# A decoder layer's early program in another order: keys of half the tokens taken together with their index queries

## The chip, the cores and the metric

The kernel runs on one core of one Trainium2 chip. The metric is device time in microseconds (us) of one execution. The core has five engines with instruction queues of their own, each worked off strictly in order: TensorE (PE in the profile, PEld for its weight loads), VectorE (DVE), ScalarE (ACT), GpSimd (POOL) and SyncE (SP), which here only issues transfers. Engines meet at semaphores. Matmuls write into PSUM banks, from which VectorE and ScalarE read.

## The reference

One decoder layer over 1024 tokens of width 1024. An adaLN modulation of the condition `c` gives shift, scale and gate; the RMS-normalised tokens times scale plus shift (`h`) go through one wide projection, whose columns feed a pooling branch and a sparse-attention branch.

```python
mod = silu(c) @ w_ada + b_ada
shift, scale, gate = split(mod, 3)
h = rmsnorm(x, norm_gain) * (1 + scale) + shift
proj = h @ w_in          # u_a z_a | q k v z_b | q_idx k_idx w_idx | g_a g_b
k, q: rmsnorm by head, partial rotary; q_idx, k_idx: partial rotary
score = sum over heads of relu(q_idx . k_idx) * w_idx    # causal; top 256 keys per query
attn = softmax over the selected keys of q . k, times v
x = x + gate * ((sigmoid(g_a) * (y_a @ w_branch_a) + sigmoid(g_b) * (y_b @ w_branch_b)) @ w_out)
```

All of it is float32.

## The kernel before

Tokens are held in 8 tiles of 128 (`NT`), channels in 8 blocks of 128 (`KD`). For float32 accuracy each operand of a large product is split into a rounded part and the remainder (`hT_hi`, `hT_lo`; `w_hi`, `w_lo`), and a product is three matmuls: hi x hi, hi x lo, lo x hi. ScalarE makes the rounded parts. VectorE makes the remainders of the tokens, and the remainders of weight pieces are made by VectorE or GpSimd (`split_piece_v`, `split_piece_lo`).

The order of the work is written out by hand, one list per engine. Three lists say who uses the PSUM banks and in which order: `pp_uses` (two banks), `pt_uses` (two, for transposes) and `ps_uses` (two double banks). A user claims a bank, which waits until the engine that read the last tenant has freed it. Weights come in pieces of 512 channels by 256 columns through three buffers `w_raw`; a load waits for the remainder of the piece three before it.

The early program, which the change rewrites, goes like this. Token tiles arrive, ScalarE takes the sum of squares of each (`square`), TensorE transposes them block by block (`h_transposes`; blocks 0 to 7 are channels of tokens 0 to 511, `f` = 0, blocks 8 to 15 those of tokens 512 to 1023, `f` = 1), and ScalarE copies the result back over `x_in` (`x_turned`). The scale part of the modulation is a product of `silu(c)` with 8 blocks of `w_ada`: VectorE folds most of them into a running sum `ada_acc` (`ada_product`), TensorE does two with one-column matmuls (`scale_columns`), and TensorE adds over partitions (`modulation_sums`). `keep_warm` is idle matmuls between them.

Keys, values, the indexer's key and its head weights (200 columns, `kv`) are computed on tokens that are scaled but not yet normalised or shifted: `scaled_hi` and `scaled_lo` make the parts, `kv_half(0)` and `kv_half(1)` do four token tiles each, ScalarE multiplies by the reciprocal root of the tile (`kv_tiles`), and a row that stands for the shift (`r`, from `shift_b`) is added to all eight tiles at once (`kr`). Meanwhile VectorE folds all 8 shift blocks (`shift_fold`), which come through four buffers `shift_w`. Only then the true tokens are made, all 16 blocks: `normalised` on VectorE, `ht_hi` on ScalarE, `ht_lo` on VectorE; the roots reach it as rows (`root_row`) by way of TensorE (`root_rows`). The index queries follow (`qi_pairs` for tiles 2, 3 and 4, 5 at 512 columns, `rows_tile` for tiles 6 and 7 at 256), then the first four tiles of q, and at L906 the index scores of block 2, which VectorE weights and sums (L2017, L2020) after it has finished the keys. Tiles 0 and 1 need no index queries, since they have at most 256 keys.

GpSimd makes the remainders of the four index-query pieces and of `wg_raw`, then the rotary of the index queries tile by tile (`rope`).

## Time and profile before

| | |
|---|---|
| median of 3 runs | 833.2 us (828.48 to 833.89) |
| profiled execution | 823.55 us |
| its span, first to last instruction | 821.8 us |
| mean granted TensorE clock in it | 0.994 of full |
| TensorE, VectorE, ScalarE, GpSimd busy | 97%, 72%, 44%, 44% of the span |

Times in all views are from the start of the span. A row of a timeline gives start, duration, engine, line, operation and, in brackets, how long the engine sat idle before it and what released it. A busy share of TensorE is of pipelined matmuls whose ends are modelled, so that starts, not durations, give the pace of a row of matmuls.

### The profile page before, as it was taken

The page shows a single profiled execution, that of the slowest core. Times are in us where ns is not written, and L with a number is a line of the kernel's source. Part 1 is how long each engine was busy: PE and PEld are TensorE (multiplying, and loading weights), DVE is VectorE, ACT ScalarE, POOL GpSimd, SP SyncE. Part 2 cuts the span into 40 slices and gives each one's busy share as a digit, 9 for nine tenths or more (in the row PEclk, how much of TensorE's full clock was granted, in tenths as well). Part 3 has the DMA queues.
Part 4 walks back from the last instruction along what each step waited for, and adds up shares of the span by engine and source line. Part 5 has one row for each costly group of instructions (what it writes and reads, how often), then busy time and mean ns, then how long its engine had stood idle before and what let it go on. Part 6 is the DMA issues. An engine that isn't in the chain of part 4 may idle for free.

```text
span 821.8 us, 12753 instructions
## 1 busy us (share of the span) xinstructions
PE 796.1 (97%) x4389; PEld 674.4 (82%) x4393; DVE 587.7 (72%) x1213; ACT 360.9 (44%) x657; POOL 358.0 (44%) x316
## 2 busy tenths in 40 slices
PE   6979999999999999999999999899999999999998
PEld 4878897888888888887778887788888887888987
DVE  5889658977888888888888716556667885772522
ACT  5866356674232222222342212587777883330100
POOL 1033844333444477852752211765888811540000
PEclk9989999999999999999999999999999999999999
DMA  9841030004242220331123321743433114753431
GB/s 343 322 140 44 7 98 14 26 14 123 93 145 65 91 79 30 97 102 52 52 76 103 103 78 67 243 143 126 134 112 109 47 27 138 256 170 123 130 101 58
DMA packets 59368, 87.87 MB, mean 107 GB/s; under 512 B 5513, under 2 KB 36525, under 8 KB 59310
## 3 DMA queue, kind: packets, MB, share of 16 engines
q1 hardware_dynamic: 47954, 65.06, 25.4%
q10 hardware_dynamic: 9436, 15.75, 5.2%
q0 software_dynamic: 1920, 6.29, 2.0%
q8 instruction: 35, 0.57, 0.3%
q14 instruction: 23, 0.19, 0.1%
HBM read 66.12 MB, written 20.97 MB: 106 GB/s over the span
## 4 chain that ended last, share of the span: by engine, by line
PE 82%; DVE 8%; ACT 3%; issue 3%; DVEq 2%; DMA 1%; POOL 1%; ACTq 0%; POOLq 0%
PE pp L720 22%; PE pp L722 21%; PE pp L721 21%; PE pp L1107 3%; PE pt L1082 3%; PE ps L906 3%; PE ps L907 3%; DVE score L2020 1%; DVE ada_acc L1822 1%; DVE hT_lo L1913 1%; DVE x_in L1906 1%; DVE hT_lo L1865 1%; DVEq L1821 1%; DMA col_rows<-in_b_ada 1%; ACT w_hi L657 1%
## 5 line engine op out<-in xcount | busy, mean ns | idle before, releaser
L662 POOL TENSOR_TENSOR w_lo<-w_raw,w_hi 128x1024 fp32r<-128x1024 f32 x45 | 111.4, 2490 | 172.8 <-ACT w_hi L657 171.3
L2045 DVE TENSOR_SCALAR_CACHE_REDUCE junk<-score,cand 128x384 uint8<-128x384 f32 (+1 forms) x186 | 168.6, 944 | 19.3 <-issue 13.3
L720 PE MATMUL pp<-hT_hi,w_hi 128*128 128x512 f32 x384 | 150.2, 391 | 0.0
L722 PE MATMUL pp<-hT_hi,w_lo 128*128 128x512 f32 x384 | 149.5, 389 | 0.0
L721 PE MATMUL pp<-hT_lo,w_hi 128*128 128x512 f32 x384 | 149.5, 389 | 0.0
L720 PEld LDWEIGHTS pp<-hT_hi,w_hi 128*128 128x128 f32 x384 | 72.1, 188 | 15.9 <-issue 0.8
L722 PEld LDWEIGHTS pp<-hT_hi,w_lo 128*128 128x128 f32 x384 | 72.1, 188 | 15.2
L721 PEld LDWEIGHTS pp<-hT_lo,w_hi 128*128 128x128 f32 x384 | 72.1, 188 | 14.8
L2108 DVE TENSOR_TENSOR pT<-pt,pT 128x512 fp32r<-128x512 f32 (+3 forms) x96 | 50.6, 555 | 45.6 <-ACT pT L1498 42.4
L1382 ACT ACTIVATE stage<-pp 128x512 f32<-128x512 f32 x32 | 19.1, 598 | 126.7 <-PE pp L722 126.7
L657 ACT ACTIVATE w_hi<-w_raw 128x1024 fp32r<-128x1024 f32 x52 | 52.8, 1053 | 44.8 <-PE pp L722 40.9
L720 PE MATMUL pp<-w_hi,hT_hi 128*128 128x256 f32 (+1 forms) x208 | 69.2, 333 | 1.0 <-ACT qi L1244 0.5
L721 PE MATMUL pp<-w_lo,hT_hi 128*128 128x256 f32 (+1 forms) x208 | 67.4, 324 | 0.0
L722 PE MATMUL pp<-w_hi,hT_lo 128*128 128x256 f32 (+1 forms) x208 | 67.4, 324 | 0.0
L720 PE MATMUL pp<-w_hi,mT_hi 128*128 128x512 f32 (+1 forms) x160 | 55.6, 348 | 0.2 <-DVE o_row L2214 0.2
L721 PE MATMUL pp<-w_lo,mT_hi 128*128 128x512 f32 (+1 forms) x160 | 55.5, 347 | 0.0
L722 PE MATMUL pp<-w_hi,mT_lo 128*128 128x512 f32 (+1 forms) x160 | 55.5, 347 | 0.0
L720 PE MATMUL pp<-yT_hi,w_hi 128*128 128x512 f32 x128 | 52.6, 411 | 0.8 <-ACT a_out L1446 0.8
L2020 DVE SCALAR_TENSOR_TENSOR score<-rel,w_idx,score 128x384 f32<-128x384 f32 (+5 forms) x42 | 45.7, 1087 | 9.0 <-ACT rel L1343 5.4
L1506 ACT ACTIVATE prob<-prob,neg_max 128x128 f32<-128x128 f32 (+7 forms) x64 | 49.8, 778 | 3.3 <-DVE neg_max L2178 2.9
L2214 DVE TENSOR_TENSOR o_row<-pp,gate 128x512 f32<-128x512 f32 (+1 forms) x20 | 11.7, 583 | 54.3 <-PE pp L722 54.3
L722 PE MATMUL pp<-yT_hi,w_lo 128*128 128x512 f32 x128 | 50.1, 392 | 0.0
(297 smaller groups left out, 1841.4 us busy)
## 6 DMA issues: line engine op xcount, KB each, us to landing
w_raw<-in_w_in SPq DMA_DIRECT2D x36, 512.0 KB, 3.7
shift_w<-in_w_ada SPq DMA_DIRECT2D x8, 512.0 KB, 6.9
sgb_spill<-stage ACTq DMA_DIRECT2D x16, 256.0 KB, 2.0
sga_spill<-stage ACTq DMA_DIRECT2D x16, 256.0 KB, 2.0
stage<-sga_spill SPq DMA_DIRECT2D x16, 256.0 KB, 3.1
ma_spill<-stage POOLq DMA_DIRECT2D x16, 256.0 KB, 2.4
gate_w<-in_w_ada SPq DMA_DIRECT2D x16, 256.0 KB, 2.7
w_raw<-in_w_out SPq DMA_DIRECT2D x8, 512.0 KB, 4.2
```

The lines of the kernel that those rows point to most:

```text
L657: nc.scalar.activation(hi, raw, ACT.Copy).then_inc(w_hi_done, 1)
L662: nc.gpsimd.tensor_tensor(lo, raw, hi.bitcast(F32), ALU.subtract).then_inc(w_lo_done, 1)
L720: nc.tensor.matmul(o, a_hi, b_hi, start=first, stop=False)
L721: nc.tensor.matmul(o, a_hi, b_lo, start=False, stop=False)
L722: return nc.tensor.matmul(o, a_lo, b_hi, start=False, stop=last)
L906: nc.tensor.matmul(o[:, a:z], q, kt_[:, 0, a:z], start=True, stop=False)
L907: last = nc.tensor.matmul(o[:, a:z], q, kt_[:, 1, a:z], start=False, stop=True)
L1082: last = nc.tensor.transpose(o[:, (t % 4) * P:(t % 4 + 1) * P], prob[j % 4][:, t * P:(t + 1) * P], ident[:])
L1506: nc.scalar.activation(prob[j % 4][:, 0:keys(b)], prob[j % 4][:, 0:keys(b)], ACT.Exp, scale=-1.0, bias=neg_max[:, j % 4:j % 4 + 1], accum_ ...
L2020: ins = v.scalar_tensor_tensor(s, rel[:, n % 2, 0:keys(b)], w, s, ALU.mult, ALU.add)
L2045: v.tensor_scalar(junk[:, n % 2, 0:keys(b)], score[:, score_at(b):score_at(b + 1)], least, None, ALU.is_ge, ALU.add, accum_out=cnt[:, n:n ...
L2108: v.tensor_tensor(pT[:, j // 2 % 2, t0:t1, 1, j % 2, :], pt[n % 2][:, 0:(t1 - t0) * P].rearrange("p (t q) -> p t q", q=P), pT[:, j // 2 % ...
```

## The change

Keys of token tiles 0 to 3 are made as before, on scaled tokens (`free_keys`), and only these four get the shift's row. Tiles 4 to 7 wait for their true tokens; then keys and index queries of the four tiles are computed together, channel block by channel block (`keys_and_queries`), keys in one double bank, two query tiles in `pp` and two in the other double bank (`qi67`). `scaled_hi`, `scaled_lo` of tokens 512 to 1023 no longer exist; the true tokens of `f` = 1 are made before those of `f` = 0. Index queries of tiles 2 and 3 come after, at 256 columns.

Around it: positions are the first load, and the angles of the rotary are computed before the column parameters arrive. Shift blocks have a place each (`shift_far` lies where half of `hT_lo` will be), so their loads wait for nothing; blocks 0 to 3 are loaded ahead of token tiles 4 to 7. TensorE does two of the shift's eight blocks (`shift_columns`, blocks 3 and 4), VectorE six. The roots of all eight tiles are taken in one step, and GpSimd copies them into `root_row`. The remainders of the four index-query pieces, of `wg_raw` and of the two pieces of q's first chunk are made by VectorE and not by GpSimd, and the index-query pieces alternate between the two chunks. ScalarE takes the sines early. Four keep-warm matmuls are left out.

```diff
+    pieces[2:6] = [(1, 0), (2, 0), (1, 1), (2, 1)]
...
-    QI_PAIRS = [2, 4]
-    QI_SINGLE = [(0, 6), (0, 7), (1, 6), (1, 7)]
-    pp_uses += [("kv", 0, t) for t in (0, 1, 4, 5)]
-    pp_uses += [("qi", BOTH, t + j) for t in QI_PAIRS for j in range(2)]
+    QI_SINGLE = [(0, 2), (0, 3), (1, 2), (1, 3)]
+    pp_uses += [("kv", 0, t) for t in (0, 1)]
+    pp_uses += [("qi", BOTH, t) for t in (4, 5)]
...
-    ps_uses = [("scale", "v"), (("kv2", 0), "a"), ("shift", "v"), (("kv2", 1), "a")]
+    ps_uses = [("scale", "v"), ("kv2", "a"), ("shift", "v"), ("kv4", "a"), ("qi67", "a"), ("r", "v")]
...
+        def shift_block(k):
+            if k < 4:
+                return shift_w[:, k, :].rearrange("p (a q) -> p a q", a=2)
+            return shift_far[:, 2 * (k - 4):2 * (k - 4) + 2, HALF:2 * HALF]
...
+            for k in range(4):
+                load_shift(k)
             for t in range(NT // 2, NT):
                 load_x(t)
-            for k in range(4):
-                load_shift(k)
-            load_piece(2)
             for k in range(4, KD):
                 load_shift(k)
-            load_piece(3)
-            load_piece(4)
+            for n in range(2, 5):
+                load_piece(n)
...
-            keep_warm(8)
+            keep_warm(4)
...
+            def shift_columns(o, i):
+                k = SHIFT_PE[i]
+                pe.wait_ge(shift_in[k], 16)
+                w = shift_block(k)
+                for j in range(KD):
+                    nc.tensor.matmul(o[:, i * KD + j:i * KD + j + 1], w[:, j // 4, (j % 4) * P:(j % 4 + 1) * P],
+                                     c_silu[:, k:k + 1], start=True, stop=True)
...
+            def keys_and_queries():
+                keys4, queries2 = ps_claim("kv4"), ps_claim("qi67")
+                o_kv = [keys4[:, (j // 2) * HALF + (j % 2) * KR_W:(j // 2) * HALF + (j % 2 + 1) * KR_W] for j in range(4)]
+                o_qi = [pp[pp_bank[pp_at[("qi", BOTH, 4 + j)]]][:] for j in range(2)]
+                o_qi += [queries2[:, 0:HALF], queries2[:, HALF:2 * HALF]]
+                first_piece = pieces_through[name_of["kv"]]
+                for k in range(KD):
+                    def tok(j):
+                        return slice((4 + j) * P, (5 + j) * P)
+                    def key_hi(j):
+                        nc.tensor.matmul(o_kv[j], hT_hi[:, k, tok(j)], kv_hi[:, k, :], start=k == 0 and j % 2 == 0, stop=False)
+                        nc.tensor.matmul(o_kv[j], hT_hi[:, k, tok(j)], kv_lo[:, k, :], start=False, stop=False)
+                    def query_hi(j):
+                        nc.tensor.matmul(o_qi[j], hT_hi[:, k, tok(j)], w_hi[:, :, k, :], start=k == 0, stop=False)
+                        nc.tensor.matmul(o_qi[j], hT_hi[:, k, tok(j)], w_lo[:, :, k, :], start=False, stop=False)
+                    def key_lo(j):
+                        return nc.tensor.matmul(o_kv[j], hT_lo[:, k, tok(j)], kv_hi[:, k, :], start=False,
+                                                stop=k == KD - 1 and j % 2 == 1)
+                    def query_lo(j):
+                        return nc.tensor.matmul(o_qi[j], hT_lo[:, k, tok(j)], w_hi[:, :, k, :], start=False,
+                                                stop=k == KD - 1)
+                    pe.wait_ge(hT_hi_done, KD + k + 1)
+                    if k == KD - 1:
+                        pe.wait_ge(hT_lo_v, KD + k + 1)
+                        for j in range(4):
+                            key_hi(j)
+                            last = key_lo(j)
+                            if j == 3:
+                                last.then_inc(ps_full, 1)
+                            query_hi(j)
+                            last = query_lo(j)
+                            if j < 2:
+                                last.then_inc(pp_full, 1)
+                            if j == 3:
+                                last.then_inc(ps_full, 1)
+                        continue
+                    for j in range(4):
+                        key_hi(j)
+                    if k % 4 == 0:
+                        pe.wait_ge(w_lo_done, first_piece + 2 * (k // 4) + 2)
+                    for j in range(4):
+                        if k == 0 and j < 2:
+                            pp_claim(("qi", BOTH, 4 + j))
+                        query_hi(j)
+                    if KD + k + 6 < 2 * KD:
+                        h_transposes(KD + k + 6)
+                    if k == 2:
+                        root_rows(0)
+                    pe.wait_ge(hT_lo_v, KD + k + 1)
+                    for j in range(4):
+                        key_lo(j)
+                        query_lo(j)
...
+            free_keys()
+            modulation = ps_claim("shift")
+            h_transposes(KD)
+            h_transposes(KD + 1)
+            shift_columns(modulation, 0)
+            h_transposes(KD + 2)
+            h_transposes(KD + 3)
+            shift_columns(modulation, 1)
+            root_rows(1)
+            modulation_sums(modulation, KD * len(SHIFT_PE), 1)
+            h_transposes(KD + 4)
+            h_transposes(KD + 5)
+            keys_and_queries()
...
+                if (i, t) == (0, 3):
+                    pe.wait_ge(shift_lo, 1)
+                    o = ps_claim("r")
+                    for k in range(KD):
+                        last = product(o[:, 0:KR_W], shift_b[:, 0, k, :], shift_b[:, 1, k, :], kv_hi[:, k, :],
+                                       kv_lo[:, k, :], k == 0, k == KD - 1)
+                    last.then_inc(ps_full, 1)
...
+            act.wait_ge(dve_ready, V_MEAN)
+            nc.scalar.activation(rx[:], ssx[:], ACT.Sqrt).then_inc(sqrt_done, 1)
+            for n in range(KD, KD + 4):
                 x_turned(n)
-                if n in ROOT_ROWS:
-                    o = pt_take(("R", ROOT_ROWS[n]))
-                    nc.scalar.activation(root_row[:, ROOT_ROWS[n], :], o[:], ACT.Copy).then_inc(pt_free_a, 1)
-                if n == KD:
-                    kv_tiles(0)
-                if n == KD + 1:
-                    split_piece_hi(act, 2)
-                if n == KD + 2:
-                    sqrt_half(1)
-                if n == KD + 5:
-                    split_piece_hi(act, 3)
+            split_piece_hi(act, 2)
+            root_taken(1)
+            free_key_tiles()
+            split_piece_hi(act, 3)
+            act.wait_ge(mod_done, 2)
+            ht_hi(KD)
+            x_turned(KD + 4)
+            x_turned(KD + 5)
+            ht_hi(KD + 1)
+            x_turned(KD + 6)
             split_piece_hi(act, 4)
-            act.wait_ge(dve_ready, V_SIN)
-            nc.scalar.activation(trig[:], reduced[:], ACT.Sin).then_inc(trig_done, 1)
-            act.wait_ge(mod_done, 2)
+            ht_hi(KD + 2)
+            x_turned(KD + 7)
+            root_taken(0)
+            ht_hi(KD + 3)
+            split_piece_hi(act, 5)
...
+            pool.wait_ge(dve_ready, V_RSQRT)
+            for f in (1, 0):
+                gp.tensor_copy(root_row[:, f, :].rearrange("p (t q) -> p t q", q=P),
+                               rx[:, 4 * f:4 * f + 4].unsqueeze(2).to_broadcast([P, 4, P])).then_inc(root_wide, 1)
...
+            FOLD_AFTER = {2: 0, 4: 1, 6: 2}
...
+            dve.wait_ge(ssx_done, NT)
+            v.tensor_scalar(ssx[:], ssx[:], 1.0 / D, EPS, ALU.mult, ALU.add).then_inc(dve_ready, 1)
+            shift_fold(5)
+            dve.wait_ge(sqrt_done, 1)
+            rsqrt_step(rx[:], ssx[:], nx[:])
+            v.tensor_copy(nx[:], rx[:]).then_inc(dve_ready, 1)
+            shift_fold(6)
+            for i in range(2):
+                shift_fold(7, (i,)).then_inc(ada_sum, 1)
...
+            split_piece_v(2)
+            normalised(KD)
+            dve.wait_ge(ps_full, ps_value("shift"))
+            sums = ps[ps_at["shift"] % 2][:, 0:PARTS * KD].rearrange("p (i j) -> p j i", i=PARTS)
+            v.tensor_reduce(shift[:, 0:KD], sums, AX.X, ALU.add).then_inc(ps_free_v, 1)
+            dve.drain()
+            v.tensor_tensor(shift[:, 0:KD], shift[:, 0:KD], col[:, 12:12 + KD], ALU.add).then_inc(mod_done, 1)
+            split_piece_v(3)
+            normalised(KD + 1)
+            ht_lo(KD)
+            normalised(KD + 2)
+            ht_lo(KD + 1)
+            split_piece_v(4)
+            normalised(KD + 3)
+            ht_lo(KD + 2)
+            split_piece_v(5)
+            normalised(KD + 4)
+            ht_lo(KD + 3)
             dve.wait_ge(shift_hi, 1)
             v.tensor_tensor(shift_b[:, 1, :, :], shift[:, 0:KD].unsqueeze(2).to_broadcast([P, KD, P]),
                             shift_b[:, 0, :, :].bitcast(F32), ALU.subtract).then_inc(shift_lo, 1)
-            for n in range(2 * KD):
-                if n + 2 < 2 * KD:
-                    normalised(n + 2)
+            for n in range(KD + 4, 2 * KD):
+                if n + 1 < 2 * KD:
+                    normalised(n + 1)
                 ht_lo(n)
+            normalised(0)
...
+            for n in range(2):
+                split_piece_v(pieces_through[name_of[("qi", 1)]] + n)
+            dve.wait_ge(ps_free_a, ps_done[ps_at["kv4"]][0])
+            dve.wait_ge(ps_full, ps_value("r"))
```

TensorE, the end of the keys on scaled tokens and what follows. Before, between the channel blocks of `kv_half(1)` (`pt` takes transposes, `ps` and `pp` the sums; L839 is the lo part of a block, L797 the shift's sums):

```order
L839 MATMUL pp<-kv_hi,hT_lo 128x200 x2
L839 MATMUL ps<-kv_hi,hT_lo 128x200 x2
L776 MATMUL pt<-ident,x_in 128x128 x4
L797 MATMUL ps<-ones,ada_acc 128x1 x8
L834 MATMUL ps<-kv_hi,hT_hi 128x200
```

Now, from the end of `free_keys` to the first of `keys_and_queries` (L868 is a key, L872 a query):

```order
L841 MATMUL ps<-kv_hi,hT_lo 128x200 x2
L785 MATMUL pt<-ident,x_in 128x128 x8
L853 MATMUL ps<-c_silu,shift_w 128x1 x8
L785 MATMUL pt<-ident,x_in 128x128 x8
L853 MATMUL ps<-c_silu,shift_far 128x1 x8
L791 MATMUL pt<-ident,root_row 128x128 x4
L806 MATMUL ps<-ones,ada_acc 128x1 x8
L785 MATMUL pt<-ident,x_in 128x128 x8
L868 MATMUL ps<-kv_hi,hT_hi 128x200
```

Transposes and sums of the second half stood between blocks of keys; now six groups of transposes, two shift products and the sums stand in one row.

SyncE, from the last load of key weights on. Before:

```order
L513 DMA w_raw<-in_w_in 128x4x128
L517 DMA x_in<-in_x 128x1024 x4
L521 DMA shift_w<-in_w_ada 128x1024 x4
L513 DMA w_raw<-in_w_in 128x4x256
L521 DMA shift_w<-in_w_ada 128x1024 x4
L513 DMA w_raw<-in_w_in 128x4x256 x2
```

Now:

```order
L522 DMA w_raw<-in_w_in 128x4x128
L528 DMA shift_w<-in_w_ada 128x1024 x4
L526 DMA x_in<-in_x 128x1024 x4
L528 DMA shift_far<-in_w_ada 128x2x512 x4
L522 DMA w_raw<-in_w_in 128x4x256 x3
```

Token tiles 4 to 7 moved behind four shift blocks, and the first query piece behind all eight.

ScalarE, the scaled blocks of channels 2 to 7 (L1248) and the squares of token tiles 4 to 7 (L1237), in the new program:

```order
L1248 ACTIVATE hT_hi<-x_in,gmul 128x512 x2
L1237 ACTIVATE w_lo,ssx<-x_in 128x1024
L1248 ACTIVATE hT_hi<-x_in,gmul 128x512
L1237 ACTIVATE w_lo,ssx<-x_in 128x1024
L1248 ACTIVATE hT_hi<-x_in,gmul 128x512
L1237 ACTIVATE w_lo,ssx<-x_in 128x1024
L1248 ACTIVATE hT_hi<-x_in,gmul 128x512 x2
L1237 ACTIVATE w_lo,ssx<-x_in 128x1024
```

Squares stand between scaled blocks as before, but their tiles now arrive behind the shift blocks, and a scaled block waits behind each.

ScalarE a little later in the new program, from the second query piece's rounded part (L663) to the fifth true block (L1253); L1243 is a turned block, L1311 the second root rows:

```order
L663 ACTIVATE w_hi<-w_raw 128x1024
L1253 ACTIVATE hT_hi<-x_in,shift 128x512
L1243 ACTIVATE x_in<-pt 128x4x128 x2
L1253 ACTIVATE hT_hi<-x_in,shift 128x512
L1243 ACTIVATE x_in<-pt 128x4x128
L663 ACTIVATE w_hi<-w_raw 128x1024
L1253 ACTIVATE hT_hi<-x_in,shift 128x512
L1243 ACTIVATE x_in<-pt 128x4x128
L1311 ACTIVATE root_row<-pt 128x512
L1253 ACTIVATE hT_hi<-x_in,shift 128x512
L663 ACTIVATE w_hi<-w_raw 128x1024
```

The turned blocks, which came one by one with a scaled block each, now stand between the true blocks, and so do the roots and two weight pieces.

## Rows read from the trace of the kernel before

**Rows 1.** waits of TensorE over the span: total us, times, longest

```profile
PE pp L839 <- DVE hT_lo L1865: 3.9, 3, 1.8
```

**Rows 2.** timeline of TensorE: start, duration, line, out<-in, count, idle before

```profile
19.28 1.07 PE L776 MATMUL pt<-ident,x_in 128*128 128x128 f32 x8
...
27.77 0.28 PE L834 MATMUL ps<-kv_hi,hT_hi 128*128 128x200 f32 x1
...
29.11 0.27 PE L834 MATMUL ps<-kv_hi,hT_hi 128*128 128x200 f32 x1
...
39.07 0.66 PE L776 MATMUL pt<-ident,x_in 128*128 128x128 f32 x4 [0.92 <-ACT kr L1235]
...
70.76 0.39 PE L874 MATMUL pp<-w_hi,hT_hi 128*128 128x512 f32 x1
...
72.12 0.39 PE L874 MATMUL pp<-w_hi,hT_hi 128*128 128x512 f32 x1
...
78.78 0.47 PE L874 MATMUL pp<-w_hi,hT_hi 128*128 128x512 f32 x1 [1.06 <-ACT qi L1244]
...
93.45 0.28 PE L720 MATMUL pp<-w_hi,hT_hi 128*128 128x256 f32 x1
...
96.33 0.46 PE L887 MATMUL pt<-ident_r,kst 128*128 128x128 f32 x4
...
115.84 0.34 PE L906 MATMUL ps<-kiT,qiT 128*128 128x384 f32 x1
```

**Rows 3.** chain that ended last, in order of time: start, us, what

```profile
21.31 1.67 PE pp L756 x7
22.99 1.69 PE ps L797 x16
...
55.05 2.83 PE ps L797 x16
...
66.13 0.66 DVE x_in L1906
```

**Rows 4.** timeline of VectorE, folds and the end of the keys

```profile
37.83 1.28 DVE L1822 SCALAR_TENSOR_TENSOR ada_acc<-shift_w,c_silu,ada_acc 128x1024 f32<-128x1024 f32 x1
...
41.98 3.29 DVE L1822 SCALAR_TENSOR_TENSOR ada_acc<-shift_w,c_silu,ada_acc 128x1024 f32<-128x1024 f32 x1
...
109.05 0.20 DVE L1805 RECIPROCAL rk<-rk 128x8 f32<-128x8 f32 x1 [13.20 <-ACT rk L1334]
...
117.44 1.10 DVE L2017 TENSOR_SCALAR score<-rel,w_idx 128x384 f32<-128x384 f32 x1 [0.57 <-ACT rel L1343]
```

**Rows 5.** timeline of GpSimd, a weight split

```profile
41.82 2.36 POOL L662 TENSOR_TENSOR w_lo<-w_raw,w_hi 128x1024 fp32r<-128x1024 f32 x1 [37.33 <-ACT w_hi L657]
```

**Rows 6.** timeline of VectorE, its start

```profile
9.84 0.21 DVE L1773 CAST pos_f<-pos_i 8x128 f32<-8x128 int32 x1 [6.71 <-DMA col_rows<-in_b_ada]
...
14.53 0.75 DVE L1820 TENSOR_SCALAR ada_acc<-scale_w,c_silu 128x1024 f32<-128x1024 f32 x1
```

**Rows 7.** windows: us, busy of PE, PEld, DVE, ACT, POOL, granted clock, DMA share, GB/s

```profile
8.00:10.00 2.00, 0.00 (x0) 0.00 (x0) 0.16 (x1) 1.84 (x5) 0.00 (x0) 1.00 1.03 415
...
52.00:54.00 2.00, 0.16 (x2) 0.08 (x1) 1.91 (x4) 0.47 (x1) 0.00 (x0) 1.00 0.48 104
...
56.00:58.00 2.00, 2.00 (x10) 2.00 (x11) 0.10 (x1) 1.98 (x3) 0.71 (x1) 0.50 0.00 0
```

**Rows 8.** DMA issues from 17 to 18 us: count, KB, us to landing

```profile
x_in<-in_x SPq DMA_DIRECT2D x1, 512.0 KB, 6.5
```

**Rows 9.** timeline of ScalarE, square and scaled block

```profile
28.65 1.04 ACT L1172 ACTIVATE hT_lo<-x_in 128x1024 fp32r<-128x1024 f32 x1
...
29.87 0.73 ACT L1191 ACTIVATE hT_hi<-x_in,gmul 128x512 fp32r<-128x512 f32 x1
30.50 1.04 ACT L1172 ACTIVATE hT_lo<-x_in 128x1024 fp32r<-128x1024 f32 x1
```

**Rows 10.** VectorE's instructions on one tile, later weight splits: ns min/median/max, first and last start

```profile
L1839 DVE TENSOR_TENSOR w_lo<-w_raw,w_hi x7: 1220/1224/1226, 193.7 to 776.8; 128x1024 fp32r<-128x1024 f32 x7
```

More of the change, by code:

```diff
@@ L226, in hybrid_layer @@
         pt_uses += [(key, "a") for key in QI_EXTRA.get(use, [])]
-    pt_uses += [(Q_EXTRA[n], "a") for n in Q_EXTRA]
+    pt_uses += [(key, "a") for n in Q_EXTRA for key in Q_EXTRA[n]]
     pt_uses += [(K_AFTER[h], "a") for h in K_AFTER]
@@ L424, in hybrid_layer @@
         ada_end = [sem(f"ada_end{i}") for i in range(2)]
[L425 removed]
+        shift_in = [sem(f"shift_in{k}") for k in range(KD)]
         mod_done, shift_hi, shift_lo = sem("mod_done"), sem("shift_hi"), sem("shift_lo")
@@ L829, in kv_half @@
-                    pe.wait_ge(hT_hi_done, KD * f + k + 1)
-                    for j in (2, 3, 0, 1):
-                        if k == 0 and j < 2:
-                            pp_claim(("kv", 0, 4 * f + j))
-                        tok = slice((4 * f + j) * P, (4 * f + j + 1) * P)
-                        nc.tensor.matmul(o[j][:, 0:KR_W], hT_hi[:, k, tok], kv_hi[:, k, :], start=k == 0, stop=False)
-                        nc.tensor.matmul(o[j][:, 0:KR_W], hT_hi[:, k, tok], kv_lo[:, k, :], start=False, stop=False)
@@ L836, in kv_half @@
-                    pe.wait_ge(hT_lo_v, KD * f + k + 1)
-                    for j in range(4):
-                        tok = slice((4 * f + j) * P, (4 * f + j + 1) * P)
-                        last = nc.tensor.matmul(o[j][:, 0:KR_W], hT_lo[:, k, tok], kv_hi[:, k, :], start=False,
+                    pe.wait_ge(hT_hi_done, k + 1)
+                    for t in (2, 3, 0, 1):
+                        if k == 0 and t < 2:
+                            pp_claim(("kv", 0, t))
+                        tok = slice(t * P, (t + 1) * P)
+                        nc.tensor.matmul(o[t][:, 0:KR_W], hT_hi[:, k, tok], kv_hi[:, k, :], start=k == 0, stop=False)
+                        nc.tensor.matmul(o[t][:, 0:KR_W], hT_hi[:, k, tok], kv_lo[:, k, :], start=False, stop=False)
@@ L840, in kv_half @@
+                    pe.wait_ge(hT_lo_v, k + 1)
+                    for t in range(4):
+                        tok = slice(t * P, (t + 1) * P)
+                        last = nc.tensor.matmul(o[t][:, 0:KR_W], hT_lo[:, k, tok], kv_hi[:, k, :], start=False,
                                                 stop=k == KD - 1)
-                        if k == KD - 1 and j < 2:
+                        if k == KD - 1 and t < 2:
                             last.then_inc(pp_full, 1)
                 last.then_inc(ps_full, 1)
+            def shift_columns(o, i):
[5 more added lines that the diff above has]
+                                     c_silu[:, k:k + 1], start=True, stop=True)
@@ L927, in _ @@
                 q_step(n)
-                if n % KD == KD - 1 and n // KD in Q_EXTRA:
-                    qi_transposes(FREE_BLOCKS, [Q_EXTRA[n // KD][2]])
+                if n % KD == KD - 1:
+                    for key in Q_EXTRA.get(n // KD, []):
+                        if key[0] == "ki":
+                            key_transposes(*key)
+                        else:
+                            qi_transposes(FREE_BLOCKS, [key[2]])
             for b in range(FREE_BLOCKS, NT):
@@ L1276, in _ @@
-            act.wait_ge(hT_lo_v, 4 * KD)
+            act.wait_ge(group_in, 16)
+            nc.scalar.activation(wg_hi[:], wg_raw[:], ACT.Copy).then_inc(wg_hi_done, 1)
+            for n in range(KD):
+                ht_hi(n)
             qi_tile(BOTH, 4)
             qi_tile(BOTH, 5)
+            late_key_tiles()
+            act.wait_ge(ps_full, ps_value("qi67"))
+            late = ps[ps_at["qi67"] % 2]
+            for j in range(2):
+                last = nc.scalar.activation(qi[:, 6 + j - FREE_BLOCKS, :], late[:, j * HALF:(j + 1) * HALF], ACT.Copy)
@@ L1280, in q_tile @@
+            last.then_inc(ps_free_a, 1)
             def q_tile(i, t):
@@ L1329, in _ @@
                 q_tile(i, t)
-                if n in Q_EXTRA:
-                    qi_copies(FREE_BLOCKS, [Q_EXTRA[n][2]])
+                for key in Q_EXTRA.get(n, []):
+                    if key[0] == "ki":
+                        key_copy(*key)
+                    else:
+                        qi_copies(FREE_BLOCKS, [key[2]])
                 if n == 0:
```

263 lines of the change are left out of this document (98 added, 165 removed).

## The prediction

> **What bounds the kernel now.** I first read the page's chain by engine, which is TensorE for the most part, then TensorE's waits. What it waits longest for on VectorE in the whole span is 3.9 us in three pieces, all in the key product, ahead of 55 us [rows 1]. From the first scores on (115.84 us [rows 2]) TensorE is close to full, and that part of the program is the same in both kernels. So the change is worth what it moves the start of the scores, if VectorE, which accumulates them, starts earlier too. I therefore rebuilt the stretch from 0 to 116 us from the timelines of the engines.
>
> In that stretch TensorE's steps have steady prices. One block of keys of four tiles is twelve matmuls, 27.77 to 29.11 us: 1.34, or 0.112 each. One block of two query tiles at 512 columns is six matmuls, 70.76 to 72.12: 1.36, or 0.227 each. One query tile at 256 columns is 93.45 to 96.33: 2.88. Two groups of f32 transposes take 1.07, a modulation product or sum with one-column matmuls (16 records) 1.69 [rows 2, 3]. VectorE's passes over a 128x512 block cost 0.66 [rows 3], a 1024-wide fold 1.28 [rows 4]. The same fold took 3.29 while GpSimd ran a weight split of 2.36 beside it [rows 4, 5]: four such splits fall into VectorE's early program.
>
> **The change part by part.** All times that follow are estimates on the clock of the profiled execution.
>
> Start. VectorE sits idle 6.71 us until 9.84 and then does some 3.4 us of angle work before its first modulation product at 14.53 [rows 6]. Positions now arrive first and the angles go into that idle time. But the products cannot gain 3.4: each wants a 0.52 MB block, and at 415 GB/s [rows 7] one lands every 1.26 us, as long as one product takes. I let them end 1 us earlier. TensorE has four keep-warm matmuls fewer (1.67 for seven: 0.95 [rows 3]), so both sides of the sum move together and the scale is ready at 24.2 and not 25.3. Bounds: 0.3 to 1.5 gained; I take 1.1.
>
> Free keys. The tokens' tiles 4 to 7 now queue on SP behind four shift blocks, 4 x 1.26 = 5 us. The first of them landed 6.5 us after its issue at about 17.1 [rows 8], at 23.6; now 28.7 to 29.4. ScalarE's squares of these tiles stand between its eight scaled blocks, and the engine comes to the first at about 27.5 (28.65 before [rows 9], less 1.1). It waits 1.2 to 1.9 there, and with it every block behind it on ScalarE, and TensorE's keys. From 29.5 ScalarE alone sets the pace: four squares at 1.22 (28.65 to 29.87) and four blocks at 0.63 (to 30.50 [rows 9]), the last block at 35.8. VectorE's last remainder and fold bring the end of the free keys to 38.4; before it was 38.15 (39.07 less 0.92 [rows 2]). The gain of the start is gone.
>
> Shift. Next TensorE does, in a row, six groups of transposes (0.53 each), one of the roots (0.4), two products of shift blocks that VectorE used to fold, and the sums: 3 x 1.69 of one-column matmuls. The sums end at 46.0. VectorE is not late: its folds 5, 6 and 7 (3.9), the roots (1.4) and the mean fit from 38.0 to 43.8. GpSimd's two root copies fall beside folds 6 and 7. No row has such a copy on GpSimd. The nearest is its split: 2.36 beside a fold that lost 2.0 [rows 4, 5], so 0 to 2 us on VectorE, of which what exceeds its slack comes on the path, at most 1.4. A copy reads one input and not two, so I stay near the low end, at 0.3. Then 0.5 for shift on VectorE and 0.65 for the first true block on ScalarE, behind its weight split: the first key matmul at 47.4.
>
> Keys and queries together. A block is 12 x 0.112 + 12 x 0.227 = 4.06, eight are 32.5, with two transposes and one of the roots 33.8. VectorE has per block two passes (1.32) and, four times in all, a split at 1.22 [rows 10], less than 4.06: TensorE sets the pace here, where VectorE did before. Two places in ScalarE's queue are new waits: turned block 14 waits for a transpose behind block 0's queries, the second roots for one behind block 2's. Behind the roots stand block 11 of the left operand, which TensorE wants at 60.3 and gets at about 60.2, and the split of the fourth query piece; behind that split stands VectorE. I take 0.4 lost, at most 0.8. End: 81.6. The blocks of the first half are finished on VectorE at about 80.2, before TensorE comes to them: no wait, with 1.4 to spare at the first tile and more at its last block.
>
> To the scores. Four query tiles, four tiles of q (8 x 2.88 = 23.0), the shift row (24 x 0.112 = 2.7), six groups of transposes at 0.3, and 0.5 for two key copies that now stand behind ScalarE's weight splits: 28.0. The hand-offs of the old order (1.06 at 78.78 [rows 2], and a shorter one) are gone, since the last block ends tile by tile. First scores at 109.6 against 115.84: **6.2 earlier**, 5.9 after GpSimd's copies.
>
> VectorE must follow. It waits for two splits of q pieces that ScalarE starts at 87.7 and for the shift row at 90; then the same key work as before runs. The key root on ScalarE comes at about 101.4 with no table load ahead of it, and VectorE needed 8.4 from there to its first score (109.05 to 117.44 [rows 4]): 109.8. Before it was ready at about the time when TensorE was, and so it is now.
>
> **The clock** is the term that no sum of works gives. Before, TensorE was busy 0.16 of 2 us from 52; then 0.50 was granted, 1.2 instead of 2.4 GHz, through the sums of one-column matmuls and into the keys [rows 7]. These sums took 2.83 instead of 1.69 [rows 3], and some 4.4 us of keys at half speed cost 2.2 more: 3.3 in all. In the new program the stretch from 38.4 to 47.4 holds 5.1 us of one-column matmuls between short transposes and ends in a wait of about a microsecond. I expect a fall here too, a shorter one: the dense matmuls come right after. Bounds 0 and 4; I take 2.
>
> The Trainium skill (TensorE: Matmul & The Clock Gate, What's actually happening) says that "the default state is throttled, and activity releases the throttle". Read as busy time, it would keep the clock up in the new stretch, where TensorE is nearly always busy, and the time would be the first rival's. The rows speak against that reading: from 56 to 58 TensorE was busy 2.00 of 2.00 us, in those very sums, at 0.50 [rows 7].
>
> **The sum.** 5.9 - 2 = 3.9 us. The profiled execution took 823.55 (span 821.8), so 819.6 there. The runs shown have their median 9.6 higher, at 833.2, and I carry the difference over: **829.3**, 0.5% faster. A difference under 1%, 8.3 us, can hardly be told from none here (the three runs lie 5.4 apart).
>
> **The rivals.**
> - The clock holds, or x tile 4 lands at the early end: 5.9 to 8 gained, 825 to 827.5. For it: the stretch has no pause as long as the 1.8 us before the old fall [rows 1]. Against it: the sums at 0.50.
> - The gain does not arrive: VectorE, not TensorE, sets when the scores go on, and its key work is delayed by GpSimd's rope passes of six blocks, which now all lie in its way from 82 to 99, or by the wait for the q splits, which stands ahead of it in its queue. With 3 to 4 us more there the gain is 0 to 2: 831 to 833. For it: VectorE's slack to the first score is only some tenths. Against it: it ran the same key work beside four rope passes before, and that is in its 8.4.
> - Slower: the late x tiles thin out the free keys so far that the clock already falls there. Keys at half speed take 2.68 a block, over ScalarE's 1.84, so four blocks lose 3.4; the shift's products and sums lose 3 x 1.14; the joint blocks 2.2. That is 9.0 against 6.2: 836. It decides from about 31 us, if the pauses there exceed 1.5 us each; I expect 0.5.
>
> **How the numbers follow.** Forecast 0.46 (2 to 5.9 gained, 827.3 to 831.2), clock holds 0.27, gain does not arrive 0.18, slower 0.09. Faster by over 1% needs 8.3 gained, beyond the best of the second case; with the spread of the runs I leave it 0.14. Slower by over 1% is the far part of the last case, 0.05. The rest, 0.81, is within 1%. For 8 in 10 the range goes from the good end of the second case, less some 1.5 for the spread of the medians, to a little beyond the third: 823.5 to 834.5.
>
> **What would show it.** Right: ScalarE's wait of over 1 us before the square of x tile 4, near 28; the free keys ending within 1 us of 38.4; the first joint block at 47 to 49; TensorE without gaps from there to 109 or 111; no 3 us folds. A granted clock of 0.50 between 42 and 52 confirms the clock's term; 1.0 there, with the scores at 109.6, is the first rival. Wrong: joint blocks longer than 4.2 us at full clock (then VectorE or ScalarE still sets the pace), TensorE waiting for VectorE at the first keys of the scores, or a fall of the clock at 30 us.

## The result and the profile after

The changed kernel took 823.29 us (median of 11 runs, 821.67 to 828.2), the kernel before 828.7 us over as many (826.43 to 833.89; the first three, shown above, happened to be high). The ratio is 0.9931 with the interval 0.9906 to 0.9956: 0.7% faster, 5.4 us. The forecast was 829.3 us with a range from 823.5, so the time lies 0.2 us below the range. The gain itself was forecast at 3.9 us.

The two profiled executions show no gain at all: 824.74 us after (span 823.0), 823.55 before. So the traces must first be compared step by step, and then it must be asked what the profiled execution of before stands for. Two rows of its TensorE, to be set beside those that follow: its pause ahead of 10 us and its first key.

```profile
10.11 0.24 PE L761 MATMUL pt<-ident,col_rows 28*128 28x28 f32 x1 [2.40 <-DVE pos_f L1773]
...
26.34 0.36 PE L834 MATMUL ps<-kv_hi,hT_hi 128*128 128x200 f32 x1 [0.57 <-DVE kv_lo L1839]
```

TensorE in the changed kernel, timeline (start, duration, line, tile, count, idle before):

```profile
4.78 3.17 PE L762 MATMUL pp<-prefix,ident_b 128*128 128x512 bf16 x7 [0.89 <-POOL rope_a L1646]
8.87 0.30 PE L771 MATMUL pt<-ident,col_rows 28*128 28x28 f32 x1 [0.92 <-DMA col_rows<-in_b_ada]
...
24.54 0.36 PE L836 MATMUL ps<-kv_hi,hT_hi 128*128 128x200 f32 x1 [0.57 <-DVE kv_lo L1907]
...
31.99 0.33 PE L836 MATMUL ps<-kv_hi,hT_hi 128*128 128x200 f32 x1 [1.84 <-ACT hT_hi L1248]
...
39.48 1.04 PE L785 MATMUL pt<-ident,x_in 128*128 128x128 f32 x8
...
46.11 3.41 PE L806 MATMUL ps<-ones,ada_acc 128*128 128x1 f32 x16
49.38 1.95 PE L785 MATMUL pt<-ident,x_in 128*128 128x128 f32 x8
50.98 0.52 PE L868 MATMUL ps<-kv_hi,hT_hi 128*128 128x200 f32 x1
...
57.18 0.26 PE L868 MATMUL ps<-kv_hi,hT_hi 128*128 128x200 f32 x1
...
61.73 0.26 PE L868 MATMUL ps<-kv_hi,hT_hi 128*128 128x200 f32 x1
...
69.91 0.36 PE L876 MATMUL ps<-kv_hi,hT_lo 128*128 128x200 f32 x1 [0.54 <-DVE hT_lo L1973]
...
87.82 0.28 PE L726 MATMUL pp<-w_hi,hT_hi 128*128 128x256 f32 x1
...
115.86 0.34 PE L963 MATMUL ps<-kiT,qiT 128*128 128x384 f32 x1
```

Between 8.87 us and the end of the early program TensorE hardly stops: the waits of [rows 1] and the hand-off of [rows 2] are gone. What is left above 0.6 us is one pause of 1.84 ahead of block 4 of the free keys. ScalarE's timeline names its cause, the late token tile, which holds the square and the scaled block behind it:

```profile
29.90 1.06 ACT L1237 ACTIVATE w_lo<-x_in 128x1024 fp32r<-128x1024 f32 x1 [2.96 <-DMA x_in<-in_x]
```

And yet the scores start at 115.86, as before [rows 2]. The windows (busy of PE, PEld, DVE, ACT, POOL, granted clock, DMA share, GB/s) show where the gain went:

```profile
30.00:32.00 2.00, 0.15 (x3) 0.04 (x1) 0.12 (x1) 1.92 (x4) 0.00 (x0) 1.00 1.01 394
...
34.00:36.00 2.00, 2.00 (x11) 2.00 (x11) 1.10 (x3) 1.92 (x4) 0.00 (x0) 0.50 1.05 387
...
42.00:44.00 2.00, 2.00 (x20) 2.00 (x21) 1.84 (x2) 1.27 (x3) 1.37 (x1) 1.00 0.11 29
44.00:46.00 2.00, 2.00 (x12) 2.00 (x12) 1.96 (x2) 0.76 (x1) 0.00 (x0) 0.52 0.00 0
...
50.00:52.00 2.00, 2.00 (x12) 2.00 (x11) 2.00 (x4) 1.84 (x4) 0.00 (x0) 0.50 0.00 0
```

The clock fell twice: after the pause, in the free keys, and again at 44.1 us, within the one-column matmuls of the shift, until 54 us. The sums took 3.27 (46.11 to 49.38) and joint block 0 took 6.20, against 4.55 for block 1. Both mechanisms were in the prediction, one as its clock term, one as the slower rival.

VectorE kept up. Its first score came 1.59 after TensorE's, before 1.60 [rows 2, 4], although two steps of eight elements, which take 0.17 elsewhere, took 1.33 and 2.27 beside two weight splits of GpSimd. Its rotary, which the second rival feared, had ended at 105.24. The kernel before has the same splits there and one such step of 2.06.

```profile
106.57 4.75 POOL L668 TENSOR_TENSOR w_lo<-w_raw,w_hi 128x1024 fp32r<-128x1024 f32 x2
...
107.67 1.33 DVE L1886 TENSOR_TENSOR nk<-rk 128x8 f32<-128x8 f32 x1
109.07 2.27 DVE L1888 TENSOR_TENSOR nk<-nk,ssk 128x8 f32<-128x8 f32 x1
...
117.45 1.10 DVE L2100 TENSOR_SCALAR score<-rel,w_idx 128x384 f32<-128x384 f32 x1 [0.87 <-ACT rel L1420]
```

Behind the first score the span has 707.1 us left, before 706.0. Most of the extra microsecond arises in one wait, at 519.68 on ScalarE's eqT (1.53; the wait at the same place before was 0.81), which stood behind a load of q rows that landed 1 us later after the same weight split. Why it landed later was not followed.

### The profile page after: what moved, and what is told of

The parts are those of the page before. It is cut to its first block, busy times and chain, and to the rows that moved or that the text cites. A ratio compares the mean times of both kernels' runs of the same rounds, so it can differ in the third digit from the quotient of the medians.

```text
span 823.0 us, 12776 instructions
## 1 busy us (share of the span) xinstructions
PE 802.8 (98%) x4421; PEld 680.7 (83%) x4421; DVE 580.0 (70%) x1201; ACT 351.6 (43%) x644; POOL 336.4 (41%) x311
## 4 chain that ended last, share of the span: by engine, by line
PE 83%; DVE 5%; ACT 4%; SPq 2%; issue 2%; DMA 2%; DVEq 1%; POOL 0%; ACTq 0%
PE pp L726 21%; PE pp L728 20%; PE pp L727 20%; PE pp L1173 3%; PE pt L1148 3%; DVE score L2103 2%; PE ps L963 2%; PE ps L964 2%; SPq L522 1%; DMA x_in<-in_x 1%; ACT w_hi L663 1%; DVE pT L2191 1%; DVE prob L2261 1%; PE pt L1081 1%; ACT rel L1420 1%
## 5 line engine op out<-in xcount | busy, mean ns | idle before, releaser
L668 POOL TENSOR_TENSOR w_lo<-w_raw,w_hi 128x1024 fp32r<-128x1024 f32 x39 | 96.4, 2487 | 122.3 <-ACT w_hi L663 121.0
L663 ACT ACTIVATE w_hi<-w_raw 128x1024 fp32r<-128x1024 f32 x52 | 52.8, 1053 | 44.6 <-PE pp L728 40.9
L1583 ACT ACTIVATE prob<-prob,neg_max 128x128 f32<-128x128 f32 (+7 forms) x64 | 49.8, 778 | 3.4 <-DVE neg_max L2261 2.9
L727 PE MATMUL pp<-yT_lo,w_hi 128*128 128x512 f32 x128 | 50.1, 391 | 0.0
```

The costliest lines, as they stand in the source:

```text
L663: nc.scalar.activation(hi, raw, ACT.Copy).then_inc(w_hi_done, 1)
L668: nc.gpsimd.tensor_tensor(lo, raw, hi.bitcast(F32), ALU.subtract).then_inc(w_lo_done, 1)
L727: nc.tensor.matmul(o, a_hi, b_lo, start=False, stop=False)
L1583: nc.scalar.activation(prob[j % 4][:, 0:keys(b)], prob[j % 4][:, 0:keys(b)], ACT.Exp, scale=-1.0, bias=neg_max[:, j % 4:j % 4 + 1], accum_ ...
```

## The experiments

The theory after this reading: the early program is shorter by about what was counted, and TensorE's clock, which falls in other places in other executions, decides what of it arrives. The rival: the 5 us lie elsewhere. Both kernels were profiled again, unchanged, beside edits.

**The kernel before, again.**

> The kernel before, unchanged, to see what an ordinary execution of it looks like: the profiled one took 823.55 us, the median of eleven is 828.7. Theory A (the two early programs differ by the works that were counted, and the rest is TensorE's clock, which falls in a different number of stretches from execution to execution): the executions at 826 to 829 have their first scores at 119 to 121 us, later than the 115.84 of the profile shown, by a longer or a second fall of the clock ahead of 116 us; mean clock 0.988 or below. Rival B (the 5 us lie elsewhere: in the scores, in the transfers, or ahead of the first instruction): first scores again near 116 us and clock near 0.994, and the added time comes after 116 us.

Median 827.34 (12 runs, 823.34 to 829.88). Its profile, of 826.33 us, has the first scores at 118.59, 2.75 later than in the execution shown and a little ahead of A's 119, and 706.0 us behind them: A and not B. But the loss is ahead of the keys, where the granted clock was 0.50 from 17.3 to 24.1 us, and the theory did not name that place: the first key is at 29.14 instead of 26.34. The executions near 828.5 have a mean clock of 0.996, higher than the quick ones (0.994), against A's 0.988. What those are was still open.

**The changed kernel, again.**

> The changed kernel, unchanged, to see how far its executions differ. Theory A: the clock falls in the keys on scaled tokens and again from the shift's products into the first joint block, as in the profile shown (first scores 115.86 us), or in only one of the two, and the first scores then come at 111 to 114; ratio to before 0.992 to 0.996. Rival B: the first scores stay within 0.5 us of 115.86 whatever the clock does, because VectorE sets them.

Median 823.58 (821.42 to 829.28); ratio 0.9945 (0.9917 to 0.9974). In this profile the fall lies in the start (the second scale product takes 3.41, first key 27.08) and in the shift (from 43.5 to 53.8 by the windows), not in the free keys; first scores 115.10, against A's 111 to 114. So where the clock falls differs between executions of one kernel.

**Tiles and shift blocks loaded in turns.**

```diff
             for k in range(4):
+                load_x(4 + k)
                 load_shift(k)
-            for t in range(NT // 2, NT):
-                load_x(t)
```

> The changed kernel with the loads of token tiles 4 to 7 and shift blocks 0 to 3 taking turns, instead of all four shift blocks ahead of the tiles. Tile 4 should land near 25 us and not 29.9. Theory A: ScalarE no longer waits 2.96 us ahead of the square of tile 4, TensorE's pause of 1.84 us at block 4 and the fall of the clock from 33.7 to 37.1 us are gone, the keys on scaled tokens end at 36 to 37 us and not 39.5, and the scores and the whole come 2 to 3 us earlier than in the changed kernel, unless VectorE's folds become late. Rival B: VectorE's folds or ScalarE set the end of the shift's sums in any case, the free keys end earlier and the sums do not: 0 to 0.5 us.

In the profile ScalarE runs from the scaled blocks into the square with no wait (first fence), TensorE's pause is gone, the free keys end at 35.71 instead of 39.48, and the scores start at 110.56. That is A's mechanism, and 5.3 us earlier, where A had 2 to 3; 3.8 of them are there at the end of the free keys. The median is 823.16 (818.82 to 828.54), 0.4 under the changed kernel on the same chip: a gain that one execution shows and twelve don't measure.

```profile
26.63 1.04 ACT L1236 ACTIVATE w_lo<-x_in 128x1024 fp32r<-128x1024 f32 x1
```

```profile
35.71 1.04 PE L784 MATMUL pt<-ident,x_in 128*128 128x128 f32 x8
...
45.40 0.52 PE L867 MATMUL ps<-kv_hi,hT_hi 128*128 128x200 f32 x1
```

**The pause of the free keys filled.**

```diff
+                    if k == 4:
+                        for _ in range(8):
+                            nc.tensor.matmul(pt[0][:], ident_b[:], prefix[:, 0:512], start=True, stop=True)
                     pe.wait_ge(hT_hi_done, k + 1)
```

> The changed kernel with eight idle matmuls of 512 columns in the pause of TensorE ahead of block 4 of the keys on scaled tokens (about 1.9 us of work in a pause of 1.84). Theory A: the pause is what lets the clock fall at 33.7 us; filled, the keys of blocks 5 and 6 run at 0.112 us a matmul and not 0.215, the free keys end 0.5 to 1 us earlier, and the whole is 0 to 1 us faster. Rival C (the fall there comes from the slow pace of the keys and not from the pause): the clock falls all the same, and the time is the same.

The profile has no fall there; the free keys run at full speed and end at 37.96. Median 823.68 (822.31 to 828.46), the same. As A says for the clock; but after_again had no fall there without the fill, so one profile does not prove it. Of all profiles of the new order this is the only one with full clock through the shift's sums (43.62 to 45.33, 1.71) and the transposes behind them, and so it shows the works that the prediction counted:

```profile
43.62 1.84 PE L806 MATMUL ps<-ones,ada_acc 128*128 128x1 f32 x16
45.33 1.07 PE L785 MATMUL pt<-ident,x_in 128*128 128x128 f32 x8
47.40 0.51 PE L871 MATMUL ps<-kv_hi,hT_hi 128*128 128x200 f32 x1 [1.00 <-ACT hT_hi L1256]
...
55.08 0.26 PE L871 MATMUL ps<-kv_hi,hT_hi 128*128 128x200 f32 x1
```

The first joint key is at 47.40, as predicted, and then block 0 takes 7.68 at half clock. From block 1 to the scores it is 58.68 in this run, in the changed kernel and in x_between alike.

**Dense matmuls between the one-column rows** (on x_between).

```diff
             shift_columns(modulation, 0)
+            dense(3)
...
             shift_columns(modulation, 1)
+            dense(3)
...
             h_transposes(KD + 5)
+            dense(3)
```

> The kernel with tiles and shift blocks loaded in turns (x_between), and three idle matmuls of 512 columns behind each of the two products of shift blocks and three ahead of the first joint block: 2.2 us more for TensorE, of which 1 us falls into the wait for the first true block. Theory A: the fall of the clock from about 43 to 49 us comes from the row of one-column matmuls; with dense work between them it does not come or comes later and shorter, the first joint block takes 4.4 us and not 6.5 in most executions, and the time is 0 to 2 us lower than that of x_between. Rival D (the fall comes from the one-column rows all the same, dense matmuls between them or not): the fall stays, and the time is 1 to 2 us higher.

Median 821.05 (818.22 to 829.88), ratio 0.9931 (0.9891 to 0.9971) against 0.9932 for x_between: no difference that can be told. In the trace the fall comes later and is shorter (46.4 to 49.8 by the windows, against 42.5 to 49.3), and block 0 takes 4.94 instead of 6.48, but counted from the end of the free keys it starts 1.7 later (11.43 against 9.69). A holds for the clock and not for the time.

**All shift blocks on VectorE** (on x_between).

```diff
-        SHIFT_PE = (3, 4)
+        SHIFT_PE = ()
...
```

> x_between with all eight shift blocks folded by VectorE, none by TensorE: 3.4 us less of one-column matmuls, 2.6 us more of folds. Theory A (the step of the prediction that VectorE is not late with six folds): the last fold ends near 44.7 us instead of 42.1, TensorE waits some 3 us for it ahead of the sums, and the first joint block starts within 1 us of that of x_between at full clock, later by 0.5 to 2; the clock falls all the same, because of the wait; time 0 to 2 us higher. Rival E (TensorE's one-column work alone set the sums): the sums end earlier, and the time is 1 to 3 us lower.

TensorE waits for the last fold, as A says, and the clock falls in that wait:

```profile
44.43 3.58 PE L805 MATMUL ps<-ones,ada_acc 128*128 128x1 f32 x16 [4.15 <-DVE ada_acc L1938]
```

Median 822.99 (821.8 to 828.14), ratio 0.9931 (0.9897 to 0.9964): the same as x_between. What TensorE saves in one-column matmuls it waits, and more: from the end of the free keys to the first joint key it is 12.78 us, against 9.69 in x_between and A's 0.5 to 2 more, and to block 1 it is 18.55 against 16.17. E falls. The two blocks on TensorE are worth 2.4 us between these two traces and nothing that the medians show.

**The kernel before, two more profiles.**

> The kernel before, unchanged: one more profile, to find an execution of the kind that takes 828 to 830 us with a mean clock of 0.996, half of all its executions. Theory A2 (TensorE's clock falls less often there, but another engine is slower in the early program): first scores at 120 to 122 us. Rival B: first scores near 116 us, and the 5 us lie behind them.

> The kernel before, unchanged: as the look before this one, for the same purpose and with the same two outcomes.

825.86 us and 829.6 us, first scores at 118.35 and 122.09: not B, and the second has A2's time. But it is no other engine that is slower there, as A2 says; it is TensorE itself. The second is of the ordinary kind. Timeline of its TensorE, and one window of its start:

```profile
4.54 3.17 PE L756 MATMUL pp<-prefix,ident_b 128*128 128x512 bf16 x7 [4.54 <-POOL rope_a L1567]
10.28 0.30 PE L761 MATMUL pt<-ident,col_rows 28*128 28x28 f32 x1 [2.57 <-DVE pos_f L1773]
...
14.26 3.41 PE L790 MATMUL ps<-c_silu,scale_w 128*128 128x1 f32 x16
...
20.22 3.41 PE L790 MATMUL ps<-c_silu,scale_w 128*128 128x1 f32 x16
...
26.62 2.89 PE L756 MATMUL pp<-prefix,ident_b 128*128 128x512 bf16 x7 [0.22 <-issue]
...
32.87 0.36 PE L834 MATMUL ps<-kv_hi,hT_hi 128*128 128x200 f32 x1 [0.58 <-DVE kv_lo L1839]
...
122.09 0.34 PE L906 MATMUL ps<-kiT,qiT 128*128 128x384 f32 x1
```

```profile
14.00:18.00 4.00, 4.00 (x21) 3.91 (x20) 3.60 (x7) 0.00 (x0) 0.00 (x0) 1.00 1.03 395
```

Both scale products take 3.41, where 1.84 is usual, and seven idle matmuls 2.89, where the execution shown has 1.67 [rows 3]. The first seven, at 4.54 or 4.78, take 3.17 in all six profiles of the two kernels. So TensorE begins at half speed, and here it stays there, through two rows of one-column matmuls, until the idle matmuls at 26.62. The first key is 6.5 us later. The clock column says 1.00 all the while: the slow start is not in it, and a mean clock of 0.996 belongs to an execution that is slower than one of 0.994.

The kernel before pauses 2.2 to 2.6 us ahead of 10 us in all four profiles, for the positions; the changed one 0.95 at most. The next four kernels ask whether that is it.

**The start of the kernel before filled, and nothing else.**

```diff
-            keep_warm(7)
+            keep_warm(13)
```

> The kernel before with 13 instead of 7 idle matmuls at its start, so that TensorE's pause of 2.2 to 2.6 us ahead of about 10 us is filled; nothing else of the change. Theory F (most of what the change gains is TensorE's speed in the first 30 us: in the profile shown the seven idle matmuls ahead of the scale's sums took 1.67 us, in the look before_fourth 2.89, with the two scale products at 3.41 each instead of 1.84, and the first key 6.5 us later; the pause is what keeps TensorE slow there): the first key comes at 26 to 27 us in the profile, the executions at 828 and above become rare, and the median falls by 2 to 5 us, to 824 to 826.5. Rival G (the speed at the start does not hang on that pause): the distribution stays, median 827 to 829.

F, inside its range: median 824.24 (822.81 to 824.95), ratio 0.9949 (0.9928 to 0.9969) to the kernel before. Above 826.5 us lie none of 12 executions; of the kernel before, on the same chip, 21 of 31.

```profile
4.54 4.75 PE L756 MATMUL pp<-prefix,ident_b 128*128 128x512 bf16 x13 [4.54 <-POOL rope_a L1567]
...
10.87 1.07 PE L776 MATMUL pt<-ident,x_in 128*128 128x128 f32 x8
...
12.42 1.84 PE L790 MATMUL ps<-c_silu,scale_w 128*128 128x1 f32 x16
...
20.30 2.43 PE L756 MATMUL pp<-prefix,ident_b 128*128 128x512 bf16 x7 [0.22 <-issue]
...
26.09 0.36 PE L834 MATMUL ps<-kv_hi,hT_hi 128*128 128x200 f32 x1 [0.58 <-DVE kv_lo L1839]
...
115.55 0.34 PE L906 MATMUL ps<-kiT,qiT 128*128 128x384 f32 x1
```

The six more take 1.58 after the first seven's 3.17: TensorE is at full speed before it pauses, and the scale products behind run at 1.84. The clock still falls afterwards in this execution, granted 0.50 from 18.4 to 21.8 us, and the idle matmuls at 20.30 took 2.43.

The fill does two things at once: it shortens the pause (to 0.85) and it makes the first row of dense matmuls longer (4.75 and not 3.17). Which of them counts was not separated, and the pause alone does not explain it. Of the six profiles of the changed kernel and its variants with seven idle matmuls and a pause of 0.95 at most, four run the eight transposes behind at half speed (1.94 us; pause_filled and dense_between after a pause of 0.27), two at full (1.07). In all three profiles with ten or thirteen idle matmuls they take 1.06 to 1.11.

**The changed kernel with the pause back.**

```diff
-            keep_warm(7)
+            keep_warm(3)
```

> The changed kernel with three instead of seven idle matmuls at its start, so that TensorE pauses about 2.6 us ahead of 8.9 us, as it did in the kernel before. Theory F: the executions at 826 and above become the most frequent, first key at 27 to 31 us, median 2 to 5 us higher than the 823.5 of the changed kernel, about level with the kernel before. Rival G: same median within 1 us.

Median 825.89 (822.95 to 830.37), 2.3 to 2.6 above the changed kernel and a ratio of 0.9979 (0.995 to 1.0008): level with the kernel before. Six of 12 lie above 826.5, against 4 of 23 of the changed kernel. F in kind; as the most frequent executions, not quite. The interval overlaps that of the changed kernel (0.9917 to 0.9974), and this edit too changes the first dense row, to three matmuls (1.46 us), with the pause: the run fits F and does not show it.

**The changed kernel with its start filled.**

```diff
-            keep_warm(7)
+            keep_warm(10)
...
-            keep_warm(4)
+            keep_warm(8)
```

> The changed kernel with ten instead of seven idle matmuls at its start (its pause there is 0.9 us) and eight instead of four ahead of the scale's sums. Theory F: executions above 826 us become rare, median 822 to 823.5; against before_start_filled it is then 1 to 4 us faster, which is what the rest of the change is worth. Rival G: the distribution stays as that of the changed kernel, or 0.5 to 1 us higher for the seven matmuls.

Median 822.17 (11 runs, 820.87 to 824.8), none above 826.5, ratio 0.9931 (0.9908 to 0.9955). F. Its scores start at 113.06, those of before_start_filled at 115.55.

```profile
24.11 0.36 PE L836 MATMUL ps<-kv_hi,hT_hi 128*128 128x200 f32 x1 [0.58 <-DVE kv_lo L1907]
...
113.06 0.34 PE L963 MATMUL ps<-kiT,qiT 128*128 128x384 f32 x1
```

The rest of the change is thus worth 2.1 us between the medians (824.24 to 822.17; the intervals of the two ratios overlap) and 2.5 between the traces. Of these 2.5, 2.0 lie ahead of the first key (26.09 against 24.11), where the clock of the other execution fell. From the first key to the scores the new order is 0.5 shorter (88.95 against 89.46), with the clock at 0.50 for 6.8 us in each, from 45.4 and from 56.0.

**Loads in turns, dense matmuls and the start filled.**

> dense_between (tiles and shift blocks loaded in turns, dense matmuls in the shift's rows) with the same fill at the start. Theory F: its four executions of twelve at 828.7 to 829.9 us disappear, the rest stays at 818 to 821.5, median 819.5 to 821. Rival G: they stay, median 821 to 822.

The executions at 828 and above are gone (818.08 to 823.8, 9 runs), but the median is 821.95, above F's range and inside that of G, whose reason fails. The ratio is 0.9921 (0.989 to 0.9951). The kernel has the lowest times of all kernels here and no median that can be told from the changed kernel's. Block 0 ends at 51.85 in its profile and at 51.88 in x_between's: the dense matmuls cost what they give.

## Why the prediction was wrong

**The step that failed** is in its sum: "The runs shown have their median 9.6 higher, at 833.2, and I carry the difference over". It took the distance between the profiled execution and the runs as a constant, outside the program and known from three runs. Neither holds.

The forecast lies 6.0 us above the measured time, and 4.5 of that is the choice of runs: over 11 runs the distance is 5.2, and the same sum would have said 824.8. No trace is of an execution of 833 or 834 us, so what makes those stays open.

And the distance is largely inside the program: it is TensorE's speed in the first 30 us, which differs between executions and which the change acts on. The prediction costed the start from one execution, in which TensorE ran at half speed only ahead of 7.7 us and from 11.0 to 14.4 us, at 1.1 us gained (0.3 to 1.5). The two profiles shown differ by 1.8 at the first key (26.34 to 24.54), but the other executions of before have it at 28.89, 29.14 and 32.87. Filling the start alone gave 4.3 us of the median (828.57 to 824.24), with nothing else of the change. With both starts filled 2.1 of the 5.4 us are left, so some 3.3 came from the start, where 1.1 was counted, and 2.1 from the rest, where 2.8 was (3.9 less 1.1). That the forecast gain of 3.9 lies no further from the measured 5.4 is luck: the two misses partly cancel. How the change quickens the start is not shown. It puts the positions first, which closes a pause of TensorE; the run with the pause back fits that, and it changed the number of idle matmuls too.

**The works** were sized well. The first key of the joint blocks was predicted at 47.4 and came at 47.40 where the clock held. A joint block with a group of transposes took 4.55, against 4.06 and 0.53. From the first joint key to the scores it is 63.2 at full clock (4.55 and 58.68), against 62.2. The 1.0 is lost in the joint blocks: 35.2 (4.55, and 57.18 to 87.82 in the changed kernel) against 34.2, of which 0.16 is a slip of the sum (32.5, twice 0.53 and 0.4 are 33.96 and not 33.8). Behind them it is 28.04 against 28.0. With both starts filled, the new early program brings 2.5 us to the scores, where 3.9 was forecast; its scores come 1.1 later than the forecast 111.9, and this 1.0 is most of that.

**The late tiles** held ScalarE longer: ScalarE waited 2.96 and not 1.2 to 1.9, since it came earlier (26.94) and the tile landed later (29.90). The free keys ended at 39.48, 38.71 and 37.96 in three profiles, against 38.4.

**The clock term** of the shift was taken as 2 us, with bounds 0 to 4. From the second shift product to block 1 the changed kernel's profile has 14.21 (42.97 to 57.18); at full clock it is 10.50 (41.45 to 47.40 in pause_filled, and 4.55). So it cost 3.7 there, 3.1 in pause_filled (7.68 less 4.55), and 2.3 and 2.2 in after_start_filled (41.61 to 54.38) and x_between (39.19 to 51.88): within the bounds, from near the 2 taken to near the upper one. The prediction's reading against the Trainium skill's "activity releases the throttle" (TensorE: Matmul & The Clock Gate, What's actually happening) was right for the sums: from 44 to 46 us TensorE was busy 2.00 of 2.00 us, at a granted 0.52. It should have been turned on the start too.

**The slower rival's mechanism** came true in the profiled execution, behind a pause of 1.84, above the 1.5 that it named, at a small price: of the blocks at half clock one took 2.62 and the next 1.77, where ScalarE's pace is 1.84.

**VectorE and GpSimd** were no bound: beside GpSimd's copies folds 6 and 7 took 3.52, where two are 2.6, and the pieces behind had slack. The wait behind the fourth query piece was 0.54, against 0.4.

## What to carry over

One profiled execution is one draw, and the median of three runs lay 4.5 us above that of eleven. Where runs of one kernel lie 8 us apart, find out in which stretch two of its own executions differ before a change is costed from one of them; a difference to the median is a term of the sum, and the change may act on it. Here idle matmuls paid before TensorE first reached full speed: six of them took 4.3 us off the median, and with both starts filled the rest of the change took off 2.1.

## What the runs showed of the hardware

TensorE begins at half speed: seven idle 512-column matmuls took 3.17 us at 4.54, and seven recorded ones of a later row 1.67 at 21.31 [rows 3]. In before_fourth, after a pause of 2.57, it stayed at half speed to beyond 27 us, while it was busy 4.00 of 4.00 us (14 to 18) with one-column matmuls and transposes, and the granted clock read 1.00. The Trainium skill (TensorE: Matmul & The Clock Gate, What's actually happening) calls the throttled state the default; the durations agree, 0.45 against 0.24 a matmul, and the profile's clock column does not show it. Where the clock falls later also differs from execution to execution of the same kernel: by the windows at 16.2 and 43.5 us in one profile of the changed kernel, at 33.8 and 44.1 in the other.
